# Recurrence stage of a two-block network: a round's 12 modulation parts in three groups of four in place of groups of two, three, three and four

## The reference, cut to what matters

```python
mod_x = (silu_c @ w_mod[layer] + b_mod[layer])[:, None, :]   # first block, 1024 x 3072
m = jax.nn.silu(cond) @ w_mod + b_mod                        # second block, per layer, 1024 x 9216
```

```python
sol = lax.linalg.triangular_solve(eye + a_mat, rhs, left_side=True, lower=True, unit_diagonal=True)
v_new = u_i - einsum(w_i, state)
o_i = einsum(q_i, state) + einsum(qk_i, v_new)
state = state * exp(gl_i) + einsum(k_i, v_new)
```

## Time and profile before

| | |
|---|---|
| median of 3 runs | 2383.66 us (2382.59 to 2388.62) |
| profiled execution, its own time | 2388.25 us |
| its span | 2386.5 us |
| PE busy | 2280.5 us (96%), 14398 instructions |
| DVE, ACT, POOL busy | 910.1, 782.9, 1024.2 us |
| recurrence, rounds 0 to 7 | about 290 to 580 us of the span |
| L593 in that stretch | 96 parts of 512 KB |

### The profile page before, as it was taken

How to read it: one execution, slowest core, us unless ns; L and a number is a source line. 1 busy time by engine, 2 the same in 40 slices (tenths; PEclk the granted TensorE clock), 3 DMA queues, 4 the chain that set the end, 5 groups by cost and what they waited for, 6 DMA issues and landing times.

```text
span 2386.5 us, 37010 instructions
## 1 busy us (share of the span) xinstructions
PE 2280.5 (96%) x14398; PEld 1821.1 (76%) x14398; DVE 910.1 (38%) x1572; ACT 782.9 (33%) x1232; POOL 1024.2 (43%) x473
## 2 busy tenths in 40 slices
PE   6999999998979999999999999999999999898999
PEld 2788877776768888878877888887888887547999
DVE  4466456655551221153372131133121124756312
ACT  2445443332232222222223223224222223424444
POOL 0446522423524444434443444443444443204888
PEclk9999999999989999999999999999999999989999
DMA  7234455545625233224323423232432322203655
GB/s 253 89 101 138 151 204 187 187 150 197 223 69 170 95 97 95 90 79 150 121 92 113 142 90 98 90 96 80 168 96 91 97 94 71 71 0 91 192 184 185
DMA packets 82682, 297.41 MB, mean 125 GB/s; under 512 B 9072, under 2 KB 11504, under 8 KB 82288
## 3 DMA queue, kind: packets, MB, share of 16 engines
q1 hardware_dynamic: 82400, 295.06, 37.7%
q10 hardware_dynamic: 144, 0.34, 0.1%
HBM read 294.31 MB, written 1.05 MB: 124 GB/s over the span
## 4 chain that ended last, share of the span: by engine, by line
issue 57%; POOL 21%; PE 18%; DVE 2%; POOLq 1%; ACT 0%; DVEq 0%; ACTq 0%
POOL w_lo L524 21%; PE bank L549 3%; PE bank L550 3%; PE bank L553 3%; PE bank L593 2%; PE bank L1379 1%; PE bank L1390 1%; PE bank L1315 1%; PE bank L894 1%; PE bank L1362 0%; DVE gdn_outer L1727 0%; PE bank L1402 0%; PE bank L1306 0%; PE bank L1413 0%; POOLq L529 0%
## 5 line engine op out<-in xcount | busy, mean ns | idle before, releaser
L524 POOL TENSOR_TENSOR w_lo<-w_raw,w_hi 128x1024 fp32r<-128x1024 f32 x383 | 931.9, 2437 | 1159.8 <-ACT w_hi L777 1159.0
L549 PE MATMUL bank<-n_hi,w_lo 128*128 128x512 f32 (+1 forms) x2216 | 792.4, 358 | 18.0 <-ACT n_hi L748 9.3
L553 PE MATMUL bank<-n_lo,w_hi 128*128 128x512 f32 (+1 forms) x2216 | 786.2, 355 | 0.6 <-DVE n_lo L701 0.3
L550 PE MATMUL bank<-n_hi,w_hi 128*128 128x512 f32 (+1 forms) x2216 | 786.3, 355 | 0.0
L777 ACT CAST w_hi<-w_raw 128x1024 fp32r<-128x1024 f32 x383 | 401.5, 1050 | 770.5 <-PE bank L553 760.3
L549 PEld LDWEIGHTS bank<-n_hi,w_lo 128*128 128x128 f32 x2216 | 420.5, 190 | 95.4 <-issue 27.9
L553 PEld LDWEIGHTS bank<-n_lo,w_hi 128*128 128x128 f32 x2216 | 420.3, 190 | 67.0 <-DVE n_lo L701 2.5
L550 PEld LDWEIGHTS bank<-n_hi,w_hi 128*128 128x128 f32 x2216 | 420.7, 190 | 63.8
L2101 DVE TENSOR_TENSOR prod<-silu,bank 128x512 f32<-128x512 f32 (+1 forms) x88 | 54.6, 622 | 723.2 <-PE bank L553 723.1
L549 PE MATMUL bank<-g_hi,w_lo 128*128 128x512 f32 (+1 forms) x768 | 283.1, 369 | 1.4 <-DVE g_lo L2092 1.4
L550 PE MATMUL bank<-g_hi,w_hi 128*128 128x512 f32 (+1 forms) x768 | 283.1, 369 | 0.0
(11 more groups left out here) (320 smaller groups left out, 1964.6 us busy)
## 6 DMA issues: line engine op xcount, KB each, us to landing
w_raw<-in_stream SPq DMA_DIRECT2D x383, 512.0 KB, 3.5
mod_raw<-in_modstream SPq DMA_DIRECT2D x64, 512.0 KB, 5.6
late<-in_modstream SPq DMA_DIRECT2D x56, 512.0 KB, 4.6
w_raw<-in_modstream SPq DMA_DIRECT2D x48, 512.0 KB, 5.7
h<-in_tokens SPq DMA_DIRECT2D x1, 2048.0 KB, 11.6
consts<-in_consts SPq DMA_DIRECT2D x1, 1152.0 KB, 9.6
h<-in_ctx SPq DMA_DIRECT2D x1, 1024.0 KB, 8.8
out<-h SPq DMA_DIRECT2D x8, 128.0 KB, 3.6
```

What stands on the lines that cost most here:

```text
L524: nc.gpsimd.tensor_tensor(w_lo[:, slot, :], w_raw[:, slot, :], w_hi[:, slot, :].bitcast(F32), ALU.subtract).then_inc(w_lo_ready, 1)
L549: nc.tensor.matmul(out_ap, wl, hi, start=start, stop=False)
L550: nc.tensor.matmul(out_ap, wh, hi, start=False, stop=False)
L553: return nc.tensor.matmul(out_ap, wh, lo, start=False, stop=stop)
```

## The change

The counts of the four groups change, the sum of 12 stays. Parts keep their order, so parts 0 and 1 of a round move from "first" to "half", part 4 moves from "half" to "last", and "key" keeps its four. The loads keep their order and their ring of 6.

```diff
-    MOD_SLOTS = {"first": 2, "half": 3, "last": 3, "key": 4}
+    MOD_SLOTS = {"first": 0, "half": 4, "last": 4, "key": 4}
     mod_copies, mod_turns = {}, {}
     m = MOD_EARLY
     for r_ in range(len(ROUNDS)):
         for slot, n_parts in MOD_SLOTS.items():
```

## The result

The changed kernel takes 2392.05 us (median of 9 runs, 2390.33 to 2394.74); the kernel before takes 2387.49 us in the runs beside it. The ratio is 1.0023 with a 95% interval of 1.0013 to 1.0033, +5.5 us on 2387.5 (3.1 to 7.9). It is slower by more than its interval, and inside the 0.3% that the prediction called no change.

What follows compares the result with a forecast made beforehand. PE was taken to bound the recurrence; -5.12 us (first), +8.08 (half and last) and +3.7 (slow second loads) gave +6.7 us, 2390.4 us from 2383.66. The 8-in-10 range was 2380 to 2397 us.

Steps and rivals of the forecast that it cites:

- PE is the bound in the recurrence: Recurrence, 306 to 580 us: PE busy 256.29 of 274.00 us; its group time counts in the span until something else is late.
- A lone part costs what a pair costs: Modulation groups: an even part and the odd one behind share their time; seven pair times a round become six.
- First gives 5.12 us: Dropping first's 1.00 us group ahead of backward L1379: 0 in round 0, 0.39 to 1.00 in others, 5.12 us off.
- The ring adds 1.52 us a round: Last's third and fourth parts wait for buffers half frees: half's start to L1505 6.94 us, +1.52 in five rounds.
- The term of +8.08: Half and last over all rounds: 7.60 in five rounds, 0.94 in round 4, -0.23 each in rounds 1 and 5.
- Slow second loads add 3.7 us: Reloads behind half's start: second loads landing later than 4.5 us after issue, 6.3 and 6.4 among eight, add 3.7 us.
- Key stays covered: Key's last load, behind last's first pair, lands 2.0 us before key begins, so it costs nothing.
- Rival 1: Last's reloads arrive in time, only gains remain: -7.5 us, 2376.2 us; chance 0.10.
- rival 2: First gives nothing because DVE or ACT is late there each round: +11.8 us, 2395.5 us; chance 0.08.
- rival 3: Slow loads in last use up key's cover in rounds 0 to 3: +10.7 us, 2394.4 us; chance 0.08.
- rival 4: New PE waits drop the clock to half speed in seven more 10 us stretches: +42 us, 2425 us; chance 0.05.
- the mechanism alone, +3.0: The forecast's first and ring terms, -5.12 and +8.08 us, without the 3.7 us of slow second loads.

Runs made afterwards that it cites:

- seven kernels with whole loads: Against before: the changed kernel; it with eight or five buffers; groups 2, 4, 2, 4; 0, 4, 2, 6; 3, 3, 3, 3; groups by round. Ratios 0.9952 to 1.0104.
- 3, 3, 3, 3: Parts in first, half, last and key set to 3 each, six buffers, against the kernel before: 2394.54 us, ratio 1.0025.
- 2, 4, 2, 4: Parts in first, half, last and key, six buffers, against the kernel before: 2381.70 us, ratio 0.9974.
- eight-buffer run: Changed kernel's groups 0, 4, 4, 4 with a ring of 8 buffers in place of 6: 2379.58 us, ratio 0.9965 against before.
- half the bytes: Changed kernel loading only 512 of 1024 columns of each recurrence part, modulation vectors not the reference's: a single run, 2384.55 us.

## Why the prediction was right, point by point

- **PE is the bound in the recurrence, and a part's time there is the span's.** Right. In all seven kernels with whole loads the sum of the two lengths moves the way the timed runs do: +5.1 and +5.5, -7.3 and -8.4, +21.9 and +24.8, -6.8 and -6.2, -9.1 and -11.5, +10.4 and +6.0, -11.1 and -11.5 us. The last key group lies behind both. The pair that is furthest apart, +10.4 and +6.0 for 3, 3, 3, 3, holds the 3.0 us of half clock in that profile.
- **A lone part costs what a pair costs.** Right. Half with four parts is as long as with three (2.69 and 2.68 us to L1495), and 2, 4, 2, 4 gains 0.84 a round.
- **First gives 5.12 us.** Right in sum, 5.3 measured, by misses that cancel in part: 0.41 and 0.40 in rounds 1 and 2 (0.39), 0.96 in round 3 (0.95). Round 4 gave 0.64 (0.39): before, a later product there ran 0.26 us longer. Rounds 5 and 6 gave 1.14 and 1.15 (1.00), 0.10 of it because L1379 starts 0.51 us behind L1390 where a part started 0.61 us behind it before, round 7 0.60 (1.00), where POOL's L1673 is late next. I had said that everything behind would move along, and had not followed POOL.
- **The ring adds 1.52 us a round.** Right. H to L1505 was forecast as 6.94 and is 6.86 to 7.02 in rounds 0, 2, 3, 5, 6 and 7; the eight-buffer run takes it away. Round 0 grew by 1.33 and not 1.52, since it was 5.69 before and not 5.42; round 1 is 7.16 and not 6.94, since its second load landed 4.7 us after issue. The term of +8.08 measured +8.0, the 10.4 less the 2.4 us of round 4's slow load. That it fits to 0.1 us is in part luck, since the misses of rounds 0 and 1, -0.19 and +0.22, cancel.
- **Slow second loads add 3.7 us.** Mis-sized. That term took two slow loads in eight from one execution; the changed kernel's profile had one in eight, 2.4 us. That is most of the step from the forecast 6.7 to the profile's 5.1. Whether it also makes the step to the timed 5.5 can't be told within an interval of 3.1 to 7.9.
- **Key stays covered.** Right: L1505 to key is 6.44 us in rounds 0 to 3 of both kernels, to 0.01, and no load is waited for in key. The cover was thinner than the 2.0 us forecast: in round 3 the load behind last's first two parts was issued at 415.9 and landed 7.2 us later, 1.0 us before key begins at 424.14.
- **Rival 1** (in time) fell with the first DMA row, **rival 2** (first gives nothing) with 5.3 us, **rival 3** (key late) with the 6.44, **rival 4** (clock) with a granted clock of 1.00 over 306 to 585 us; it showed once elsewhere, in the profile of 3, 3, 3, 3. I put 0.51 on slower than 2390.8 and 0.41 on within; on the same median of before, 2383.66, the measured ratio gives 2389.1. The slow loads had pushed the forecast to the border, and the mechanism alone, +3.0, lay well inside.

What stays open is what makes a second load slow. SP's issue was long for each of the three slow ones (765 to 1312 ns in place of 431). A long issue alone is not it: with half the bytes, second loads whose issue took 653 to 1077 ns landed after 3.4 to 4.1 us, the others after 3.2 to 3.9. No run tells the cause.

## What to carry to other kernels

When filler work is moved between places in an engine's order, count the buffers that two neighbouring places use together. Here the ring was invisible as long as the sum stayed within it (6 of 6, 8 of 8). Two parts beyond it put an issue and a landing of 4.4 us on the chain, of which 1.5 us a round stood out, at a mean DMA share of only 0.49. Group filler so that matmuls that can share the array start together, and put it where the engine waits anyway; here 0, 4, 2 and 6 with the same ring is 11.5 us faster than before, where 0, 4, 4 and 4 is 5.5 slower. And a wait between two parts that each use half of the strips hardly shows as idle time; look for groups that have split.

## What was not expected of the hardware

- The second load of a burst, issued 0.37 us after the first, lands 1.3 us after it at 512 KB (3.6 and then 4.5 us from issue) and 1.7 us after it with half the bytes (2.6 and then 3.9); over the eight rounds with half the bytes it is 1.0 to 1.9 us. Halving the bytes of queued loads did not shorten their spacing.
- Of the second loads behind H, two in eight took 6.3 and 6.4 us to land before, one in eight 6.9 in the changed kernel; all others took 4.3 to 4.7.
- In the changed kernel PE was granted its full clock from 306 to 585 us (1.00), with waits for loads of up to 1.87 us in round 4; after the wait of 4.65 us ahead of L1379 in round 0 it ran at half clock for some 10 us (0.68 over 290 to 306 us), as before. With groups of 3, 3, 3, 3 it ran at half clock over 491 to 497 us (0.50) behind waits of only 0.35 and 0.78 us.
- In the changed kernel a 64x64 left product started 0.51 us behind the start of a right product of the same shape (round 5, 470.54 to 471.05). The same right product was followed after 0.61 us when the next matmul had another shape: a 128x128 one there (472.16 to 472.77), a 128x32 part before (427.50 to 428.11).
